# Odd K/V weight slabs: the low-part subtraction on GpSimd instead of VectorE, and the gated norm's squares taken step by step

## The chip, the cores and the metric

The kernel runs on one core of one Trainium2 chip. The metric is the device time of one execution in microseconds. Three runs of the kernel before gave 1953.63, 1960.84 and 1962.93 us (median 1960.84 us).

## What is computed

One layer of a hybrid decoder for 256 prompt tokens and 8 x 4 sample tokens (288 columns, T). A combined input projection feeds three mixers (conformer convolution, S5, Mamba-2 SSD), then come the output projection, cross-attention over 256 memory tokens, and a convolutional FFN. What matters here, cut from the reference:

```python
memn = _rmsnorm(mem_prompt, norm_mem_w[l])
mk = (memn @ xa_wk[l]).reshape(bp, N_MEM, XA_HEADS, XA_HEAD_DIM)
mv = (memn @ xa_wv[l]).reshape(bp, N_MEM, XA_HEADS, XA_HEAD_DIM)
...
y = y.reshape(bt, L, D_C) * jax.nn.silu(z.astype(f32))
yg = y.reshape(bt, L, SSD_GROUPS, D_C // SSD_GROUPS)
yg = yg * lax.rsqrt(jnp.mean(yg * yg, axis=-1, keepdims=True) + EPS)
```

## The kernel before

**The K/V stage.** The products with `xa_wk` and `xa_wv` are computed in 64 weight slabs (`y` = 0 to 63, eight groups of eight; a slab is 128 x 1024 elements). Each weight is split in a high and a low part of type fp32r: `hi` is the rounded copy, `lo` = weight - `hi`. Per slab, ScalarE (ACT) copies `raw` to `khi` (`k_split`, L1566), VectorE (DVE) subtracts `khi` from `raw` into `raw_lo` (`k_split`, L2286), and TensorE (PE) does 12 matmuls in `kv_group`: high x high, high x low (`raw_lo`) and low activations x high, for two tiles of memory tokens. `khi` has two buffers, so ACT writes slab y only when PE is done with slab y-2 (`wait_used_A`); `raw` and `raw_lo` have four. PE waits once per slab, on `kw_lo`, before its first matmul of the slab.

**What is woven in.** Between slabs PE runs hooks (`hook_kv`) with the work of the SSD mixer. For head pair j (0 to 7) the SSD's steps stand at fixed slabs, given by `ssd_at`: `ssd_a(j)` after slab 12+6j, `ssd_b(j)` after slab 15+6j. Each engine has its own queue in program order, written out by hand. ACT and DVE have a loop over y with `k_split(y + 1)` at the head of step y, and the SSD's operations behind it. On ACT, `ssd_decay(j)` (exponentials, L1641, L1643) is at step 13+6j, `ssd_states(j)` at 14+6j; at step 13+6j the load of the next state waits for a store (`st_ssd`).

**GpSimd (POOL)** has two plain loops for this stage. The first runs over j: `dec` x `cb` (L640) and `decs` x `cbs` (L643) twice, when ACT has made the exponentials, then the state times its decay (L649). The second, behind it, runs over j again: the square of the gated tile `zs` (L656) and its addition to `ssq` or `sqt` (L657), each waiting for `gated`, which DVE signals in `ssd_b(j)` at step 15+6j. PE's `gate_sums` (after slab 60) needs all squares. POOL does nothing else between the S5 mixer's products (L624, L626) and the memset behind the gate sums (L670).

**Other names.** At step 5 DVE makes `xds` (L2337, `token_rows(2)`), which PE's `chunk_state(0)` multiplies after slab 6. The first two slabs of `w_out`, y = 64 and 65, are also split by `k_split` into `khi` and `raw_lo`.

Of the kernel before, what the change touches and what calls it, by code (L numbers as in the profile page):

```python
# [6 lines left out]
F32 = mybir.dt.float32  # L7
F32R = mybir.dt.float32r
ALU = mybir.AluOpType
# [23 lines left out]
YT = NH * HP // P  # L33
# [59 lines left out]
def hymba_step(nc, I, O):  # L93
# [3 lines left out]
    def S(name):  # L97
        name = PLACE.get(name, (name, 0))[0]
        if name not in sems:
            sems[name] = ctx.enter_context(nc.semaphore(name))  # L100
        return sems[name]

    def at(name, count):

        return S(name), count + PLACE.get(name, (name, 0))[1]
# [4 lines left out]
    with ctx:  # L110

        def sb(name, shape, dt=F32):
            return alloc(ctx, name, shape, dt)
# [21 lines left out]
        raw_lo = alloc(lev, "raw_lo", [P, 4, 1024], F32R)  # L135
        lev.close()
        raw = sb("raw", [P, 4, 1024])
# [22 lines left out]
        khi = alloc(lev, "khi", [P, 2, 1024], F32R)  # L160
# [178 lines left out]
        NKV = 8 * 8  # L339
# [27 lines left out]
        def ssd_at(y, first):  # L367

            j, r = divmod(y - first, SSD_STEP)
            return j if r == 0 and 0 <= j < YT else None  # L370
# [195 lines left out]
        def _(pool):  # L566
# [66 lines left out]
            me.link(pool.memset(sqt[:, :], 0.0))  # L633


            for j in range(YT):
                g = j // 4
                for h in range(2):
                    pool.wait_ge(*at("decay", 4 * j + 2 * h + 1))
                    pool.tensor_tensor(vsplit(dec[:, h, :], 2), vsplit(dec[:, h, :], 2),  # L640
                                       cb[:, :, g, :], ALU.mult).then_inc(S("mixed"), 1)
                    pool.wait_ge(*at("decay", 4 * j + 2 * h + 2))
                    pool.tensor_tensor(decs[:, h, :], decs[:, h, :], cbs[:, g, :], ALU.mult)\  # L643
                        .then_inc(S("mixed"), 1)

                pool.wait_ge(*at("eb_ready", j + 1))
                pool.wait_ge(*at("s0_T", 2 * j + 2))
                last = eb[:, P:P + NS].rearrange("p (b l) -> p b l", l=NL)[:, :, NL - 1]
                pool.tensor_tensor(s0[:, j % 2, :, :], s0[:, j % 2, :, :],  # L649
                                   last.unsqueeze(2).to_broadcast([P, NB, NST]), ALU.mult)\  # L650
                    .then_inc(S("s0_decayed"), 1)

            for j in range(YT):
                pool.wait_ge(*at("gated", j + 1))
                dst = ssq if j < 4 else sqt
                me.link(pool.tensor_tensor(hbuf[:, 1, :], zs[:, j, :], zs[:, j, :], ALU.mult))  # L656
                q = pool.tensor_tensor(dst[:, :], dst[:, :], hbuf[:, 1, :], ALU.add)  # L657
                if j % 4 == 3:
                    q.then_inc(S("gate_sq"), 1)
                    pool.wait_ge(*at("gate_sq", j // 4 + 1))  # L660
                else:
                    me.link(q)


            for n, ready in enumerate(("x_out", "x_o", "x_down")):
                if n == 0:
                    pool.wait_ge(*at("gate_mm", 2))
# [28 lines left out]
        def _(pe):  # L696
# [288 lines left out]
            def kv_group(g, hook):  # L985
                for s in range(8):
                    sl = NA + 8 * g + s
                    pe.wait_ge(*at("kw_lo", 8 * g + s + 1))
                    wh = khi[:, sl % 2, :].rearrange("p (k n) -> p k n", k=2)
                    wl = raw_lo[:, sl % 4, :].rearrange("p (k n) -> p k n", k=2)  # L990
                    for t in range(MT):
                        if s == 0 and g > 0:
                            pe.wait_ge(*at("kv_read", 2 * (g - 1) + t + 1))
                        if s == 0 and g == 0:
                            pe.wait_ge(*at("in_read", 28 + t + 1))
                        for kk in range(2):
                            k = 2 * s + kk
                            if g == 0 and t == 0:
                                pe.wait_ge(*at("m_lo", k + 1))
                            xh, xl = mhi[:, k, t * P:(t + 1) * P], mlo[:, k, t * P:(t + 1) * P]  # L1000
                            mm(B[t][:, :], xh, wh[:, kk, :], k == 0, False)
                            mm(B[t][:, :], xh, wl[:, kk, :], False, False)
                            q = mm(B[t][:, :], xl, wh[:, kk, :], False, k == KT - 1)
                        if s == 7:
                            q.then_inc(S("kv_acc"), 1)
                    if s < 7:
                        q.then_inc(S("kv_slab"), 1)
                    hook(8 * g + s)
# [912 lines left out]
        def _(v):  # L1921
# [361 lines left out]
            def k_split(y):  # L2283

                v.wait_ge(*at("kw_hi", y + 1) if y < NKV else at("w_hi", y - NKV + 1))
                tt(raw_lo[:, y % 4, :], raw[:, y % 4, :], khi[:, y % 2, :].bitcast(F32), ALU.subtract)\  # L2286
                    .then_inc(S("kw_lo" if y < NKV else "w_lo"), 1)
# [123 lines left out]
                    ALU.mult, ALU.mult).then_inc(S("gate_scaled"), 1)  # L2411

            for y in range(NKV):
                k_split(y + 1)
                if y < 4:
                    mem_lo(8 + 2 * y)
                    mem_lo(9 + 2 * y)
                conf_end(y)
                if y == TOKENS_AT + 1:
                    token_columns()  # L2420
                if TOKENS_AT + 2 <= y < TOKENS_AT + 5:
                    token_rows(y - TOKENS_AT - 2)
                if y in (STATES_AT, STATES_AT + 1):
                    chunk_state(y - STATES_AT)
                if y == STATES_AT + 2:
                    final_state()
                if y == CB_AT:
                    c_b()
                if y == CB_AT + 1:
                    sample_tokens()  # L2430
                j = ssd_at(y, SSD_AT)
                if j is not None:
                    ssd_a(j)
                j = ssd_at(y, SSD_AT + SSD_HALF)
                if j is not None:
                    ssd_b(j)
                j = ssd_at(y, SSD_AT + SSD_HALF + 1)
                if j is not None:
                    ssd_update(j)
                if y == GATE_AT:  # L2440
                    for g in range(2):
                        v.wait_ge(*at("gate_mm", g + 1))
                        if g == 0:
                            v.wait_ge(*at("gated", YT))
                        ts(rstd[:, :] if g == 0 else hbuf[:, 0, :], B[2 + g][:, 0:T], 1.0 / 512, EPS,
                           ALU.mult, ALU.add).then_inc(S("gate_read"), 1)
                if y in (GATE_AT + 1, GATE_AT + 2):
                    gate_root(y - GATE_AT - 1)
                if y == NKV - 1:
                    for j in range(4):  # L2450
                        gate_scale(j)
# [304 lines left out]
```

## Time and profile before

| | |
|---|---|
| median of three runs | 1960.84 us |
| the profiled execution, whole time | 1955.62 us |
| its span | 1953.6 us |
| PE busy | 1893.7 us (97%) |
| DVE busy | 1088.5 us (56%) |
| ACT busy | 703.8 us (36%) |
| POOL busy | 235.2 us (12%) |

Everything is read from one profiled execution. Its span runs from its first to its last instruction; 2.0 us of the whole time lie around it. A wait is put down to the operation that released it last. Matmuls are pipelined, so that a row of 0.39 us is followed by the next 0.23 us later. PEclk is TensorE's granted clock, 1.00 for 2.4 GHz and 0.50 for 1.2 GHz. The timeline has one row for an instruction or a run of like ones: start, length, engine, line, operation, output <- inputs, count, and in brackets how long the engine sat idle before it and who ended that.

### The profile page before, as it was taken

How to read it: one execution, taken by the hardware profiler on the slowest of the kernel's cores; microseconds unless marked ns; L12 is line 12 of the kernel's file. 1: busy time of each engine (PE TensorE's matmuls, PEld its weight loads, DVE VectorE, ACT ScalarE, POOL GpSimd, SP SyncE). 2: the span in 40 equal slices, each digit the busy share in tenths (PEclk: the TensorE clock that was granted, in tenths of full speed). 3: DMA queues.
4: the chain of work that ended last, by engine and by line, in shares of the span. 5: the costliest groups of instructions: out<-in, count | busy, mean ns of one | idle time of the engine just before them, and what ended most of it. 6: DMA issues, size and time to landing. Idle time of an engine off the chain costs nothing.

```text
span 1953.6 us, 32075 instructions
## 1 busy us (share of the span) xinstructions
PE 1893.7 (97%) x12311; PEld 1690.9 (87%) x12311; DVE 1088.5 (56%) x1923; ACT 703.8 (36%) x1051; POOL 235.2 (12%) x257
## 2 busy tenths in 40 slices
PE   7999999799999999999999999999999999999998
PEld 4866677677777799996599999999999999999997
DVE  4796697564444546444334655555555554555554
ACT  2100152533333334324223444444444434444444
POOL 1023200001122233000013100000000000002300
PEclk9999999999999899999999999999999999999999
DMA  6333363355455646646745455555555555554553
GB/s 203 98 97 91 93 199 110 99 161 163 153 169 172 210 154 218 223 159 259 294 136 163 149 164 167 165 161 163 166 165 161 163 157 162 160 163 156 160 166 105
DMA packets 157953, 316.43 MB, mean 162 GB/s; under 512 B 16938, under 2 KB 39482, under 8 KB 152931
## 3 DMA queue, kind: packets, MB, share of 16 engines
q1 hardware_dynamic: 136146, 296.01, 48.6%
q10 hardware_dynamic: 21723, 19.27, 3.1%
q8 instruction: 56, 0.92, 0.2%
q14 instruction: 28, 0.23, 0.0%
HBM read 300.78 MB, written 14.89 MB: 162 GB/s over the span
## 4 chain that ended last, share of the span: by engine, by line
PE 86%; DVE 3%; ACT 2%; DMA 1%; issue 0%; ACTq 0%; SPq 0%; DVEq 0%
PE bank L698 23%; PE bank L1119 19%; PE bank L1121 19%; PE bank L1120 19%; PE bank L1219 2%; PE bank L1231 1%; PE bank L767 1%; PE bank L752 1%; DVE wlo L2459 1%; PE bank L1241 1%; DVE raw_lo L2286 1%; DMA raw<-in_w_out 1%; PE bank L1062 0%; DMA kv<-in_cache_mem_v 0%; DVE hlo L2481 0%
## 5 line engine op out<-in xcount | busy, mean ns | idle before, releaser
L1119 PE MATMUL bank<-hhi,whi 128*128 128x288 f32 x2128 | 635.4, 299 | 13.0 <-DVE wlo L2459 9.8
L1120 PE MATMUL bank<-hlo,whi 128*128 128x288 f32 x2128 | 632.0, 297 | 0.0
L1121 PE MATMUL bank<-hhi,wlo 128*128 128x288 f32 x2128 | 629.8, 296 | 0.0
L2459 DVE TENSOR_TENSOR wlo<-raw,whi 128x1024 fp32r<-128x1024 f32 (+1 forms) x270 | 330.3, 1224 | 390.0 <-ACT whi L1612 389.7
L1612 ACT ACTIVATE whi<-raw 128x1024 fp32r<-128x1024 f32 (+1 forms) x270 | 283.2, 1049 | 520.8 <-PE bank L1121 509.2
L1119 PEld LDWEIGHTS bank<-hhi,whi 128*128 128x128 f32 x2128 | 402.1, 189 | 14.9 <-DVE wlo L2459 14.6
L1121 PEld LDWEIGHTS bank<-hhi,wlo 128*128 128x128 f32 x2128 | 404.6, 190 | 0.0
L1120 PEld LDWEIGHTS bank<-hlo,whi 128*128 128x128 f32 x2128 | 402.9, 189 | 0.1
L698 PE MATMUL bank<-hT,raw 128*128 128x288 f32 x1024 | 264.7, 418 | 1.2 <-DVE hT L1946 1.2
L698 PEld LDWEIGHTS bank<-hT,raw 128*128 128x128 f32 x1024 | 196.9, 195 | 60.4 <-issue 7.4
L1119 PE MATMUL bank<-ahi,whi 128*128 128x288 f32 x688 | 204.3, 297 | 3.5 <-DVE alo L2696 1.6
L1120 PE MATMUL bank<-alo,whi 128*128 128x288 f32 x688 | 203.5, 296 | 0.0
L1121 PE MATMUL bank<-ahi,wlo 128*128 128x288 f32 x688 | 203.5, 296 | 0.0
L2693 DVE TENSOR_TENSOR wlo<-raw,whi 128x1024 fp32r<-128x1024 f32 x86 | 106.4, 1238 | 137.2 <-ACT whi L1888 137.1
L1888 ACT ACTIVATE whi<-raw 128x1024 fp32r<-128x1024 f32 x86 | 91.2, 1060 | 159.6 <-PE bank L1121 159.6
L2286 DVE TENSOR_TENSOR raw_lo<-raw,khi 128x1024 fp32r<-128x1024 f32 x66 | 86.6, 1312 | 93.2 <-ACT khi L1566 93.0
L1119 PEld LDWEIGHTS bank<-ahi,whi 128*128 128x128 f32 x688 | 129.3, 188 | 4.8 <-issue 2.8
L1120 PEld LDWEIGHTS bank<-alo,whi 128*128 128x128 f32 x688 | 129.3, 188 | 0.0
L1121 PEld LDWEIGHTS bank<-ahi,wlo 128*128 128x128 f32 x688 | 129.3, 188 | 0.0
L698 PE MATMUL bank<-khi,mhi 128*128 128x512 f32 x256 | 112.4, 439 | 13.0 <-DVE raw_lo L2286 12.9
L1566 ACT ACTIVATE khi<-raw 128x1024 fp32r<-128x1024 f32 x66 | 69.8, 1058 | 150.2 <-PE bank L698 146.3
L698 PE MATMUL bank<-raw_lo,mhi 128*128 128x512 f32 x256 | 106.6, 416 | 0.0
(474 smaller groups left out, 1978.9 us busy)
## 6 DMA issues: line engine op xcount, KB each, us to landing
raw<-in_ffn_w_down SPq DMA_DIRECT2D x86, 512.0 KB, 3.7
raw<-in_ffn_w_gate SPq DMA_DIRECT2D x80, 512.0 KB, 3.6
raw<-in_ffn_w_up SPq DMA_DIRECT2D x80, 512.0 KB, 3.6
raw<-in_w_in SPq DMA_DIRECT2D x64, 512.0 KB, 3.6
raw<-in_xa_wk SPq DMA_DIRECT2D x32, 512.0 KB, 3.8
raw<-in_xa_wv SPq DMA_DIRECT2D x32, 512.0 KB, 4.4
raw<-in_w_out SPq DMA_DIRECT2D x32, 512.0 KB, 3.8
raw<-in_xa_wq SPq DMA_DIRECT2D x32, 512.0 KB, 3.8
```

The costliest lines, as they stand in the source:

```text
L698: return pe.matmul(out, lhsT=l, rhs=r, start=start, stop=stop)
L752: q = pe.matmul(B[4 + j % 2][:, i * NP:(i + 1) * NP], lhsT=l, rhs=uT[r:r + 32, j // 4, 0:NP], start=True, stop=True, tile_position=(r, 0))
L1119: pe.matmul(out, lhsT=wh[:, wo:wo + P], rhs=xh, start=first, stop=False)
L1120: pe.matmul(out, lhsT=wh[:, wo:wo + P], rhs=xl, start=False, stop=False)
L1121: return pe.matmul(out, lhsT=wl[:, wo:wo + P], rhs=xh, start=False, stop=last)
L1219: x = pe.transpose(B[5 + u % 3][:, hh * NM + t * P:hh * NM + (t + 1) * P], cache(b)[:, t, c0:c0 + P], ident[:, :])
L1566: a(khi[:, y % 2, :], raw[:, y % 4, :], ACT.Copy).then_inc(S("kw_hi" if y < NKV else "w_hi"), 1)
L1612: a(whi[:, slot, 0:2 * width], raw[:, s % 4, 0:2 * width], ACT.Copy).then_inc(S("w_hi"), 1)
L1888: a(whi[:, slot, :], raw[:, n % 4, :], ACT.Copy).then_inc(S("w_hi"), 1)
L2286: tt(raw_lo[:, y % 4, :], raw[:, y % 4, :], khi[:, y % 2, :].bitcast(F32), ALU.subtract)\
L2459: tt(wlo[:, s % 2, wsl], raw[:, s % 4, wsl], whi[:, s % 2, wsl].bitcast(F32), ALU.subtract)\
L2693: tt(wlo[:, slot, :], raw[:, (NB_DOWN + base + j) % 4, :], whi[:, slot, :].bitcast(F32), ALU.subtract).then_inc(S("w_lo"), 1)
```

## The change

The subtractions `raw_lo` = `raw` - `khi` of the odd slabs (y = 1, 3, ... 63) are issued on POOL and leave DVE; the even ones stay. PE waits for `kw_lo_pool` at odd slabs and for `kw_lo` at even ones. POOL's two loops over j become one loop over y, with the SSD's steps at the slabs of the other engines' loops: `k_split` of the next slab at even steps, `ssd_mix(j)` at 13+6j, `s0_decay(j)` at 14+6j, `gate_square(j)` at 16+6j. The arithmetic is the same.

```diff
--- before.py
+++ after.py
@@ -633,7 +633,13 @@
             me.link(pool.memset(sqt[:, :], 0.0))
 
 
-            for j in range(YT):
+            def k_split(y):
+
+                pool.wait_ge(*at("kw_hi", y + 1))
+                pool.tensor_tensor(raw_lo[:, y % 4, :], raw[:, y % 4, :], khi[:, y % 2, :].bitcast(F32),
+                                   ALU.subtract).then_inc(S("kw_lo_pool"), 1)
+
+            def ssd_mix(j):
                 g = j // 4
                 for h in range(2):
                     pool.wait_ge(*at("decay", 4 * j + 2 * h + 1))
@@ -643,6 +649,7 @@
                     pool.tensor_tensor(decs[:, h, :], decs[:, h, :], cbs[:, g, :], ALU.mult)\
                         .then_inc(S("mixed"), 1)
 
+            def s0_decay(j):
                 pool.wait_ge(*at("eb_ready", j + 1))
                 pool.wait_ge(*at("s0_T", 2 * j + 2))
                 last = eb[:, P:P + NS].rearrange("p (b l) -> p b l", l=NL)[:, :, NL - 1]
@@ -650,7 +657,7 @@
                                    last.unsqueeze(2).to_broadcast([P, NB, NST]), ALU.mult)\
                     .then_inc(S("s0_decayed"), 1)
 
-            for j in range(YT):
+            def gate_square(j):
                 pool.wait_ge(*at("gated", j + 1))
                 dst = ssq if j < 4 else sqt
                 me.link(pool.tensor_tensor(hbuf[:, 1, :], zs[:, j, :], zs[:, j, :], ALU.mult))
@@ -661,7 +668,18 @@
                 else:
                     me.link(q)
 
-
+            for y in range(NKV - 1):
+                if y % 2 == 0:
+                    k_split(y + 1)
+                j = ssd_at(y, SSD_AT + 1)
+                if j is not None:
+                    ssd_mix(j)
+                j = ssd_at(y, SSD_AT + 2)
+                if j is not None:
+                    s0_decay(j)
+                j = ssd_at(y, SSD_AT + SSD_HALF + 1)
+                if j is not None:
+                    gate_square(j)
             for n, ready in enumerate(("x_out", "x_o", "x_down")):
                 if n == 0:
                     pool.wait_ge(*at("gate_mm", 2))
@@ -985,7 +1003,7 @@
             def kv_group(g, hook):
                 for s in range(8):
                     sl = NA + 8 * g + s
-                    pe.wait_ge(*at("kw_lo", 8 * g + s + 1))
+                    pe.wait_ge(*at("kw_lo_pool" if s % 2 else "kw_lo", (8 * g + s) // 2 + 1))
                     wh = khi[:, sl % 2, :].rearrange("p (k n) -> p k n", k=2)
                     wl = raw_lo[:, sl % 4, :].rearrange("p (k n) -> p k n", k=2)
                     for t in range(MT):
@@ -2411,7 +2429,8 @@
                     ALU.mult, ALU.mult).then_inc(S("gate_scaled"), 1)
 
             for y in range(NKV):
-                k_split(y + 1)
+                if y % 2:
+                    k_split(y + 1)
                 if y < 4:
                     mem_lo(8 + 2 * y)
                     mem_lo(9 + 2 * y)
```

## Rows read from the trace of the kernel before

**Rows 1.** Windows view, K/V stage: window, length, PE PEld DVE ACT POOL, PEclk, DMA, GB/s.
```profile
361.80:662.50 300.70, 284.15 (x1294) 213.71 (x1292) 151.08 (x218) 118.35 (x191) 51.80 (x57) 0.93 0.49 152
```

**Rows 2.** Waits of PE, 355 to 670 us: total us, times, longest.
```profile
PE bank L698 <- DVE raw_lo L2286: 12.9, 7, 5.5
PE bank L1119 <- DVE raw_lo L2286: 0.7, 1, 0.7
```

**Rows 3.** Timeline, slabs 27 and 28: start us, length us, engine, operation.
```profile
487.90 1.04 ACT L1566 ACTIVATE khi<-raw 128x1024 fp32r<-128x1024 f32 x1
489.12 1.22 POOL L643 TENSOR_TENSOR decs<-decs,cbs 32x32 f32<-32x32 f32 x1
490.32 1.91 POOL L649 TENSOR_TENSOR s<-s,eb 128x1024 f32<-128x1024 f32 x1
488.98 1.26 DVE L2286 TENSOR_TENSOR raw_lo<-raw,khi 128x1024 fp32r<-128x1024 f32 x1 [4.07 <-ACT khi L1566]
491.06 2.25 DVE L2286 TENSOR_TENSOR raw_lo<-raw,khi 128x1024 fp32r<-128x1024 f32 x1 [0.82 <-ACT khi L1566]
```

**Rows 4.** Timeline of PE: first matmul of slabs 1, 27, 33, 57 and 60.
```profile
368.56 0.50 PE L698 MATMUL bank<-khi,mhi 128*128 128x512 f32 x1 [0.86 <-DVE raw_lo L2286]
490.30 0.50 PE L698 MATMUL bank<-khi,mhi 128*128 128x512 f32 x1 [0.85 <-DVE raw_lo L2286]
520.20 0.50 PE L698 MATMUL bank<-khi,mhi 128*128 128x512 f32 x1 [2.02 <-DVE raw_lo L2286]
631.54 0.50 PE L698 MATMUL bank<-khi,mhi 128*128 128x512 f32 x1 [1.53 <-DVE raw_lo L2286]
649.44 0.50 PE L698 MATMUL bank<-khi,mhi 128*128 128x512 f32 x1 [0.27 <-DVE raw_lo L2286]
```

**Rows 5.** The subtractions on DVE: ns min/median/max, first and last start.
```profile
L2286 DVE TENSOR_TENSOR raw_lo<-raw,khi x66: 1201/1226/2248, 362.9 to 664.0; 128x1024 fp32r<-128x1024 f32 x66
```

**Rows 6.** The same view of five operations on POOL.
```profile
L643 POOL TENSOR_TENSOR decs<-decs,cbs x16: 242/244/1229, 430.9 to 630.4; 32x32 f32<-32x32 f32 x16
L640 POOL TENSOR_TENSOR dec<-dec,cb x16: 714/730/2027, 430.1 to 629.7; 128x256 f32<-128x256 f32 x16
L603 POOL TENSOR_TENSOR sqt<-xT x40: 666/668/1592, 692.8 to 1810.0; 128x288 f32<-128x288 f32 x40
L624 POOL TENSOR_TENSOR hAB<-gri,tabC x16: 1262/1264/1278, 128.7 to 229.4; 128x512 f32<-128x512 f32 x16
L649 POOL TENSOR_TENSOR s<-s,eb x8: 1905/1911/1919, 434.9 to 631.6; 128x1024 f32<-128x1024 f32 x8
```

**Rows 7.** Timeline near 642 us: DVE reading a PSUM bank beside POOL.
```profile
641.94 1.27 DVE L2400 TENSOR_TENSOR s<-bank,s 128x512 f32<-128x512 f32 x2
642.62 0.80 POOL L657 TENSOR_TENSOR sqt<-sqt,hbuf 128x288 f32<-128x288 f32 x1
```

**Rows 8.** Timeline, slab 15: ACT, DVE, PE.
```profile
432.57 1.06 ACT L1566 ACTIVATE khi<-raw 128x1024 fp32r<-128x1024 f32 x1 [2.06 <-PE bank L698]
433.66 1.23 DVE L2286 TENSOR_TENSOR raw_lo<-raw,khi 128x1024 fp32r<-128x1024 f32 x1 [3.31 <-ACT khi L1566]
435.11 0.40 PE L698 MATMUL bank<-khi,mhi 128*128 128x512 f32 x1
```

**Rows 9.** Timeline around the first chunk state: ACT, DVE, PE.
```profile
399.68 1.06 ACT L1566 ACTIVATE khi<-raw 128x1024 fp32r<-128x1024 f32 x1 [2.83 <-PE bank L698]
401.60 1.20 DVE L2337 TENSOR_TENSOR xds<-xdt,tokT 128x1024 f32<-128x1024 f32 x1
403.31 1.02 PE L698 MATMUL bank<-xds,btok 128*128 128x512 f32 x2
```

**Rows 10.** PE's wait in w_out; windows behind it and behind slab 33's start.
```profile
678.51 0.40 PE L1119 MATMUL bank<-hhi,whi 128*128 128x288 f32 x1 [2.98 <-DVE wlo L2459]
680.00:683.30 3.30, 3.30 (x15) 3.30 (x15) 0.00 (x0) 0.00 (x0) 0.00 (x0) 0.50 0.93 294
520.20:523.00 2.80, 2.80 (x12) 2.17 (x12) 2.03 (x1) 0.74 (x1) 1.92 (x2) 1.00 1.07 349
```

## The prediction

> **What bounds the kernel now.** First the busy shares of the page (the table above): TensorE (PE) 97%, everything else under 60%. Next the windows view of the K/V stage, slabs 0 to 63, the only part that the change touches: PE is busy for 284 of 300.7 us, DVE for 151, ACT for 118, POOL for 52 [rows 1]. So the stage is PE's, and DVE's busy time is worth nothing in itself. The waits of PE come third: those for L2286 are 12.9 us in seven in the stage and 0.7 us in one at the first slab of w_out [rows 2]. No wait of PE for POOL stands in that view. The timeline then tells what these waits are. At slabs 27, 33 and 57 `khi` itself is late (ACT had other work), and `raw_lo` follows at once: at slab 27 `khi` ends at 488.94, DVE subtracts from 488.98 to 490.24, PE starts at 490.30 [rows 3, 4]. None of the seven comes from DVE being busy with something else (at slab 60 its subtraction itself was held up, below); where DVE's queue held a subtraction back, PE had time in hand. The length of the subtraction itself is on PE's path wherever little time lies between the end of `khi` and PE's need.
>
> **The price of the new operation.** On DVE 66 subtractions take 1.226 us in the median [rows 5]. POOL does none of this kind in the trace. Its rows with two different full inputs are 0.730 us for 256 elements and 1.264 us for 512 [rows 6]: 2.09 ns an element and about 0.2 us fixed, which gives 1.264 + 512 x 0.00209 = 2.33 us for 1024. A row with 1024 elements is there, L649, at 1.911 us, but its second input is one value for 128 elements each; the square L603, both of whose inputs are the same tile, is cheap in the same way (0.668 us at 288, where the line of the other two gives 0.80). I take 2.33 us, since `raw` and `khi` differ in each element, and keep 1.91 as the lower end. Lower than that nothing in the trace suggests. The output type fp32r has no row on POOL, and neither has the way from POOL to PE; the trace has 0.04 us from ACT to DVE and 0.05 from DVE to PE [rows 3, 4], and I allow up to 0.15 more per hand-over as the upper end.
>
> The Trainium skill, "GPSIMD Engine Reference", section 3.1, has 4497 ns for a `tensor_tensor` add of 2048 fp32 elements on GpSimd, against 2293 on DVE. Half of it, 2.25 us, would be an estimate from that page for this operation; by it the ten delays below would each be 0.08 us shorter and the sum 0.8 us less. No run here shows that figure.
>
> **Who blocks whom.** At slab 27 POOL's small product starts at 489.12 and ends at 490.34, 0.10 us behind DVE's subtraction, where its median is 0.244 us [rows 3, 6]. Then DVE's subtraction of slab 28 starts at 491.06 and ends at 493.31, 1.08 us behind POOL's 490.32 to 492.23; it takes 2.25 us instead of 1.23 [rows 3]. So one stands still until the other is through. Both DVE subtractions read two tiles in SBUF. An operation of DVE that reads a PSUM bank and one SBUF tile, at 641.94, runs beside POOL's at 642.62, and both have their usual length (1.27 us for two, 0.80) [rows 7]; so I count collisions only where DVE reads two SBUF tiles. The Trainium skill, "SBUF — State Buffer", section "Who interferes with whom", says that a DVE instruction contends with a GpSimd one that reads SBUF if both its own inputs lie in SBUF; the rows agree; it speaks against this change, and without it the 0.9 us for `xds` below would fall away.
>
> **The change part by part.** Removed from DVE: 32 subtractions, 39 us, all beside PE's work: nothing. Added on POOL: 32 x 2.33 = 75 us, in a stage of 300 us where POOL has 52. What counts is each odd slab whose time from the end of `khi` to PE's start is less than 0.03 + 2.33 + 0.05 = 2.41 us. I went through all 32.
>
> - Slabs 1 and 3: PE already waits 0.86 and 5.5 us for DVE's result [rows 2, 4]. Each wait grows by 2.33 - 1.23 = 1.10 us: +2.2 us.
> - Slabs 15, 21, 39, 45: two slabs stand back to back without a hook between them. At slab 15 `khi` ends at 433.63, DVE is through at 434.89 and PE starts at 435.11, without a wait [rows 8]. The time is 1.48 us there and 1.45 to 1.49 at the other three. Each becomes a wait of 2.41 - 1.48 = 0.93 us: +3.7 us.
> - Slabs 27, 33, 51, 57: `khi` follows ACT's exponentials directly, and on POOL `ssd_mix(j)` stands ahead of `k_split(15+6j)`. At slab 27 its last product starts at 489.12 and takes 0.24 us when DVE is out of the way, so POOL is free at 489.36, 0.42 us behind the end of `khi`. The subtraction then ends at about 491.72 and PE starts at 491.77 instead of 490.30 [rows 3, 4]: +1.47 us. The same working gives 1.46 to 1.48 at 33, 51 and 57: +5.9 us. This is the only place where the order of POOL's queue costs something.
> - Slab 63: the same 1.48 us as slab 15, so +0.93; but slab 64, whose subtraction DVE can start earlier without slab 63's, had a wait of 0.7 us [rows 2] that absorbs most of it, while slab 65's `khi` hangs on slab 63's end and comes late. I take +0.5 us (0.05 to 0.93).
> - The first chunk state: `khi` of slab 7 ends at 400.74, so POOL works until 400.77 + 2.33 = 403.10. DVE's `xds`, two inputs in SBUF, wants to run from 401.60 to 402.80 and now ends 1.08 us behind POOL, at 404.18; PE wants it at 403.31 [rows 9]: +0.9 us.
> - The other odd slabs have 2.46 us or more and wait for nothing (25 and 49, at 2.46 to 2.48, have under 0.1 us to spare). DVE's subtraction for the next even slab may be held back behind POOL's at 16+6j, but those slabs have over 7 us.
> - The squares: 16 POOL operations leave the stretch 633 to 648 us and stand one by one behind `gated`. Behind `gate_square(j)` on POOL waits only slab 19+6j, whose `khi` comes 8 us later. What is won is the wait at slab 60, 0.27 us [rows 4], since there the squares held DVE's subtraction up: -0.27 us. No DMA and nothing on SP's queue moves.
>
> Nothing takes a delay back in between: what `khi` waits for is PE's own progress (`wait_used_A`), and the state's store is issued by PE's progress too. Sum: 2.2 + 3.7 + 5.9 + 0.5 + 0.9 - 0.3 = 12.9 us.
>
> **The clock.** After PE's wait of 2.98 us in w_out the granted clock was 0.50 from 680.0 to 683.3; after slab 33's 2.02 us it stayed at 1.00 [rows 10]. The waits at slabs 33 and 57 grow to about 3.5 and 3.0 us. A stretch of 3.4 us at half speed costs 1.7 us. I count one of the two: +1.7 us; bounds none and three (5.1 us).
>
> The forecast is +14.6 us: 1955.6 + 14.6 = 1970.2 us for the profiled execution. The median of the runs lies 5.2 us above that execution, so 1960.8 + 14.6 = 1975.4 us.
>
> **Rivals.**
> (a) *The subtraction costs POOL what L649 costs.* With 1.91 us the terms are 2 x 0.68, 4 x 0.51, 4 x 1.05, 0.45, 0.2 and -0.27: +8.0 us without a fall of the clock, 1968.9 us. For it: the only row of that size. Against it: the line through 256 and 512 elements, and L603.
> (b) *Relief of DVE decides, faster.* Where DVE does other work after `khi`, POOL starts at once; and the waits at slabs 60 and 64 go, 0.27 + 0.7 = 1.0 us [rows 2, 4]. That comes out ahead only if POOL's subtraction takes less than about 1.4 us, so that slabs 15 to 63 keep their cover: 1959.8 us. Against it: the rows of POOL at 512 elements and more [rows 6].
> (c) *Collisions breed more waits.* POOL is now busy for 75 us more, and each DVE operation with two SBUF inputs that meets it is held by up to 2.3 us; each hand-over costs 0.15 us more, slabs 25, 49 and 61 begin to wait, and the clock falls three times instead of once: 12.9 + 1.5 + 0.5 + 5.1 = +20.0 us, 1980.8 us. For it: the waits sit beside the hooks in which the clock falls already.
> That the change doesn't do what it says is no rival here: the line of each subtraction is fixed by the program.
>
> **Numbers.** Forecast 0.60, (a) 0.21, (b) 0.04, (c) 0.15. The range takes in (a) and (c) and, at each end, 3 us for the scatter of the runs (1953.6 to 1962.9): 1965 to 1984. About 0.5%, 9.8 us, is what a measurement of this kernel can tell from no change. The forecast and (c) lie beyond it, (a) within: slower 0.73, same 0.24, faster 0.03.
>
> **What would show it.** Right: POOL has 32 subtractions of about 2.3 us; PE's waits for POOL's subtraction stand at slabs 1, 3, 15, 21, 27, 33, 39, 45, 51, 57 and 63 and grow to 23 us or so with what was there; those at 27, 33 and 57 are 2.3, 3.5 and 3.0 us; PE waits some 0.9 us for `xds` near 405 us; slab 60 has no wait. The stage, 300.7 us, becomes 313 to 316 us, and what lies before and behind it keeps its length. Wrong: subtractions of 1.9 us or less (then it is (a)), or waits at slabs 5, 9, 17 or 23, which I hold to be covered.

## The result

The changed kernel takes 1983.4 us (median of four runs, 1981.9 to 1989.4) against 1961.9 us: the ratio is 1.0124, with a 95% interval of 1.0089 to 1.0159, slower by 17 to 31 us. Measured again beside others it was 1981.5 us (1972.1 to 1986.1, five runs), ratio 1.0096 (1.0080 to 1.0111). A ratio is taken over all the runs, not from the two medians (21.5 us apart in the first measurement). The forecast was +14.6 us; the first ratio stands for +24.3 us, the second for +18.8.

The page of the changed kernel, its first and its fourth part. Line numbers have moved: L716 is L698 of before, L1584 is L1566, L2304 is L2286, and POOL's subtraction is L639.

```profile
PE 1908.5 (96%) x12311; PEld 1698.5 (86%) x12311; DVE 1064.3 (54%) x1891; ACT 703.7 (36%) x1051; POOL 305.8 (15%) x289
PE bank L716 22%; PE bank L1137 19%; PE bank L1139 18%; PE bank L1138 18%; PE bank L1237 2%; POOL raw_lo L639 1%; PE bank L1249 1%; PE bank L770 1%; PE bank L785 1%; DMA out_s_ssd<-s 1%; DVE wlo L2478 1%; PE bank L1259 1%; DMA raw<-in_w_out 1%; PE bank L1080 0%; ACT khi L1584 0%
```

(The first line: busy us and share of each engine; the second: shares of the span by line in the chain that ended last.) POOL has 306 us of work instead of 235. DVE has only 24 us less, though 32 subtractions of 1.226 us, 39 us, have left it: those that are left take 1.68 us each in the mean of the stage, as some stand behind POOL's operations (below). POOL's `raw_lo` now stands in the chain with 1%. PE is busy for 1908.5 us instead of 1893.7, with the same 12311 instructions.

The windows view (window, length, busy us of PE, PEld, DVE, ACT, POOL, granted clock, DMA share, GB/s) of the kernel before and then of the changed one, each cut at the first `khi` and at the first matmul of w_out. The first line of the kernel before answers to [rows 1] with that cut.

```profile
361.80:662.56 300.76, 284.15 (x1295) 213.75 (x1293) 151.14 (x218) 118.35 (x191) 51.80 (x57) 0.93 0.49 152
0.00:361.80 361.80, 347.36 (x1505) 254.71 (x1506) 257.77 (x663) 70.39 (x142) 46.52 (x65) 0.98 0.42 128
662.56:1999.00 1336.44, 1262.17 (x9514) 1222.44 (x9514) 679.62 (x1043) 515.04 (x719) 136.88 (x135) 0.99 0.54 168
```

```profile
361.88:691.33 329.45, 299.64 (x1294) 222.10 (x1293) 127.79 (x188) 118.27 (x191) 122.11 (x89) 0.89 0.45 139
0.00:361.88 361.88, 346.66 (x1505) 254.13 (x1506) 257.78 (x663) 70.42 (x142) 46.57 (x65) 0.98 0.42 128
691.33:1999.00 1307.67, 1262.20 (x9514) 1222.28 (x9514) 678.71 (x1040) 514.99 (x719) 137.10 (x135) 0.99 0.55 172
```

(The last window runs past the end of the span.) The loss lies in the K/V stage alone: 300.8 us became 329.5 us, and the stretches before and behind it kept their length (361.8 and 361.9; 1291.0 and 1290.6 to the end). Inside the stage PE is idle for 329.45 - 299.64 = 29.8 us, where it was 300.76 - 284.15 = 16.6: +13.2 us. And it is busy for 15.5 us more with the same matmuls, at a granted clock of 0.89 instead of 0.93.

The second measurement has a profile of the changed kernel too. Its K/V stage:

```profile
360.76:682.23 321.47, 292.02 (x1295) 216.55 (x1293) 127.77 (x188) 118.25 (x191) 122.12 (x89) 0.91 0.46 143
```

Here the stage takes 8.0 us less than in the first profile, with as much idle time (29.5 us) and 7.6 us less of busy time, at a clock of 0.91. So the idle time is the kernel's, while the clock's part differs from one execution to the next.

The waits of PE (total us, times, longest), which answer to [rows 2]:

```profile
PE bank L716 <- POOL raw_lo L639: 23.3, 12, 6.4
PE bank L716 <- DVE raw_lo L2304: 1.9, 1, 1.9
PE bank L716 <- DVE xds L2355: 0.9, 1, 0.9
PE bank L1137 <- issue: 0.7, 1, 0.7
```

12.9 us in the stage became 23.3 + 1.9 + 0.9 = 26.1 us: +13.2, the idle time just found. The wait for `xds` is new. (DVE's 1.9 us, at slab 0, was in the 12.9 us already.)

POOL's subtraction (ns min/median/max), beside [rows 5, 6], and its collision at slab 9:

```profile
L639 POOL TENSOR_TENSOR raw_lo<-raw,khi x32: 2337/2367/2979, 367.5 to 685.1; 128x1024 fp32r<-128x1024 f32 x32
414.26 2.98 POOL L639 TENSOR_TENSOR raw_lo<-raw,khi 128x1024 fp32r<-128x1024 f32 x1 [8.19 <-ACT khi L1584]
```

2.37 us in the median, and never under 2.34. POOL started 0.07 to 0.14 us behind the end of `khi` where it was free, DVE 0.04 us [rows 3].

The timeline (start, length, engine, line, operation): the chunk state, beside [rows 9]; slab 15, beside [rows 8]; slab 27 and the start of slab 33, beside [rows 3, 4]:

```profile
404.45 2.71 DVE L2355 TENSOR_TENSOR xds<-xdt,tokT 128x1024 f32<-128x1024 f32 x1
407.21 1.13 PE L716 MATMUL bank<-xds,btok 128*128 128x512 f32 x2 [0.89 <-DVE xds L2355]
...
436.37 1.06 ACT L1584 ACTIVATE khi<-raw 128x1024 fp32r<-128x1024 f32 x1 [2.06 <-PE bank L716]
439.95 0.50 PE L716 MATMUL bank<-khi,mhi 128*128 128x512 f32 x1 [0.88 <-POOL raw_lo L639]
...
497.50 1.04 ACT L1584 ACTIVATE khi<-raw 128x1024 fp32r<-128x1024 f32 x1
498.73 0.24 POOL L649 TENSOR_TENSOR decs<-decs,cbs 32x32 f32<-32x32 f32 x1
498.94 2.34 POOL L639 TENSOR_TENSOR raw_lo<-raw,khi 128x1024 fp32r<-128x1024 f32 x1
501.24 1.90 POOL L656 TENSOR_TENSOR s<-s,eb 128x1024 f32<-128x1024 f32 x1
500.65 3.58 DVE L2304 TENSOR_TENSOR raw_lo<-raw,khi 128x1024 fp32r<-128x1024 f32 x1 [6.46 <-ACT khi L1584]
501.33 0.50 PE L716 MATMUL bank<-khi,mhi 128*128 128x512 f32 x1 [2.34 <-POOL raw_lo L639]
...
534.17 0.80 PE L716 MATMUL bank<-khi,mhi 128*128 128x512 f32 x1 [3.46 <-POOL raw_lo L639]
```

At slab 27 `khi` ends at 498.54, POOL is still at its last product until 498.94, and PE starts 2.34 us late; at slab 33 it is 3.46 us, at slab 15 0.88 us. DVE's `xds` took 2.71 us instead of 1.20, as POOL's subtraction of slab 7 (403.67 to 406.07) was in the way. The 3.58 us of DVE's subtraction for slab 28 are the same thing: it ends 1.09 us behind POOL's state product (501.24 to 503.14). PE did not need it yet.

The clock behind the waits, in the windows view: behind the start of slab 27, behind that of slab 33 and in the slab behind the next hook. The third number from the end is the granted clock.

```profile
501.00:505.00 4.00, 3.67 (x10) 2.91 (x11) 3.23 (x1) 0.00 (x0) 2.15 (x2) 0.62 0.33 124
534.20:540.00 5.80, 5.80 (x16) 4.18 (x16) 2.88 (x1) 0.24 (x1) 1.79 (x1) 0.54 0.23 84
547.30:553.00 5.70, 5.70 (x15) 4.44 (x15) 2.41 (x3) 0.13 (x1) 0.00 (x0) 0.50 0.00 0
```

Behind the wait of 3.46 us PE worked at or near 1.2 GHz (0.54) for slab 33's twelve matmuls, where the kernel before had 1.00 at the same place [rows 10]. Behind 2.34 us it was 0.62. Yet a wait alone does not settle the clock. The second profile of the changed kernel, behind the same wait at slab 33 (3.45 us):

```profile
532.70:538.50 5.80, 5.80 (x35) 4.60 (x36) 2.90 (x1) 1.06 (x1) 3.37 (x2) 1.00 0.47 156
```

And slab 0, where nothing has changed yet and both kernels wait alike (1.88 us before, 1.89 now): the stretch from its start in the kernel before, then in the changed one, and the changed kernel's slab 1.

```profile
364.20:368.50 4.30, 3.47 (x16) 2.67 (x16) 3.63 (x7) 3.81 (x9) 0.00 (x0) 1.00 0.03 5
364.30:368.60 4.30, 4.30 (x12) 3.29 (x13) 2.44 (x6) 3.03 (x7) 1.13 (x1) 0.64 0.00 0
369.89 0.50 PE L716 MATMUL bank<-khi,mhi 128*128 128x512 f32 x1 [0.53 <-POOL raw_lo L639]
```

The same length of wait was followed by full speed once and by the low clock once. At slab 1 the slow matmuls of slab 0 took up most of the time for which PE would have waited: 0.53 us are left, while the slab starts 2.56 us behind the end of its `khi` instead of 1.31 us.

### The profile page after: what moved, and what is told of

The parts are those of the page before. It is cut to its first block, busy times and chain, and to the rows that moved or that the text cites. A ratio compares the mean times of both kernels' runs of the same rounds, so it can differ in the third digit from the quotient of the medians.

```text
span 1981.9 us, 32075 instructions
## 1 busy us (share of the span) xinstructions
PE 1908.5 (96%) x12311; PEld 1698.5 (86%) x12311; DVE 1064.3 (54%) x1891; ACT 703.7 (36%) x1051; POOL 305.8 (15%) x289
## 4 chain that ended last, share of the span: by engine, by line
PE 85%; DVE 2%; ACT 2%; POOL 2%; DMA 2%; issue 1%; ACTq 0%; SPq 0%; DVEq 0%; POOLq 0%
PE bank L716 22%; PE bank L1137 19%; PE bank L1139 18%; PE bank L1138 18%; PE bank L1237 2%; POOL raw_lo L639 1%; PE bank L1249 1%; PE bank L770 1%; PE bank L785 1%; DMA out_s_ssd<-s 1%; DVE wlo L2478 1%; PE bank L1259 1%; DMA raw<-in_w_out 1%; PE bank L1080 0%; ACT khi L1584 0%
## 5 line engine op out<-in xcount | busy, mean ns | idle before, releaser
L1137 PE MATMUL bank<-hhi,whi 128*128 128x288 f32 x2128 | 634.7, 298 | 12.9 <-DVE wlo L2478 9.8
L1137 PEld LDWEIGHTS bank<-hhi,whi 128*128 128x128 f32 x2128 | 401.9, 189 | 14.9 <-DVE wlo L2478 14.6
L716 PE MATMUL bank<-hT,raw 128*128 128x288 f32 x1024 | 263.1, 415 | 1.2 <-DVE hT L1964 1.2
L716 PEld LDWEIGHTS bank<-hT,raw 128*128 128x128 f32 x1024 | 195.6, 194 | 60.1 <-issue 7.4
L716 PE MATMUL bank<-khi,mhi 128*128 128x512 f32 x256 | 117.6, 460 | 25.3 <-POOL raw_lo L639 23.3
L1584 ACT ACTIVATE khi<-raw 128x1024 fp32r<-128x1024 f32 x66 | 69.8, 1057 | 169.7 <-PE bank L716 165.8
L639 POOL TENSOR_TENSOR raw_lo<-raw,khi 128x1024 fp32r<-128x1024 f32 x32 | 76.4, 2389 | 290.3 <-ACT khi L1584 290.3
L694 POOL TENSOR_TENSOR cg<-cg,rstd 128x288 f32<-128x288 f32 x43 | 42.9, 998 | 482.9 <-ACT cg L1856 482.9
```

Of the source, the lines that this page charges most:

```text
L639: pool.tensor_tensor(raw_lo[:, y % 4, :], raw[:, y % 4, :], khi[:, y % 2, :].bitcast(F32), ALU.subtract).then_inc(S("kw_lo_pool"), 1)
L694: pool.tensor_tensor(cg[:, m, :], cg[:, m, :], rstd[:, :], ALU.mult)\
L716: return pe.matmul(out, lhsT=l, rhs=r, start=start, stop=stop)
L1137: pe.matmul(out, lhsT=wh[:, wo:wo + P], rhs=xh, start=first, stop=False)
L1584: a(khi[:, y % 2, :], raw[:, y % 4, :], ACT.Copy).then_inc(S("kw_hi" if y < NKV else "w_hi"), 1)
```

## The experiments

For the experiments a second measure helps. Each run of each kernel has its span and its mean granted clock. Their product is the time that the run would take at full clock, if all of it scaled; the remainder of the span is what the clock cost. (A wait that falls into a stretch at half clock counts at half its length there, so the split is not exact.) The means over the runs of each kernel, with the standard error in brackets:

| kernel | runs | median us | ratio to before (95%) | span x clock | clock's cost |
|---|---|---|---|---|---|
| before | 54 | 1962.6 | 1 | 1914.3 (0.2) | 46.9 (0.6) |
| changed (both measurements) | 9 | 1982.3 | see above | 1926.1 (0.6) | 54.1 (2) |
| squares alone | 10 | 1961.1 | 0.9978 (0.9958 to 0.9998) | 1912.7 (0.7) | 45.4 (1.4) |
| longer on VectorE | 4 | 1987.1 | 1.0126 (1.0109 to 1.0143) | 1927.0 (1.0) | 59.1 (1.7) |
| waits filled | 4 | 1977.8 | 1.0075 (1.0054 to 1.0096) | 1928.4 (1.0) | 46.9 (1.9) |
| twelve slabs on VectorE | 10 | 1959.0 | 0.9985 (0.9971 to 0.9999) | 1914.6 (0.5) | 43.3 (1.2) |
| high parts first, GpSimd | 12 | 1954.1 | 0.9957 (0.9939 to 0.9975) | 1911.1 (0.5) | 40.7 (0.9) |
| high parts first, VectorE | 6 | 1950.6 | 0.9944 (0.9923 to 0.9965) | 1908.0 (0.4) | 40.6 (1.3) |
| split before mix | 4 | 1983.2 | 1.0114 (1.0088 to 1.0140) | 1924.5 (0.8) | 56.5 (1.9) |
| before, filled | 10 | 1961.5 | 1.0001 (0.9983 to 1.0019) | 1920.1 (0.4) | 40.6 (0.9) |
| four late slabs on VectorE | 6 | 1971.2 | 1.0041 (1.0027 to 1.0056) | 1921.4 (0.7) | 47.6 (1.6) |
| seven short ones on VectorE | 7 | 1972.8 | 1.0046 (1.0023 to 1.0069) | 1918.9 (0.7) | 51.2 (2.3) |

So over nine runs the change costs 11.8 us of full-clock time and 7.2 (2) us of clock. In the one profiled pair the clock's part looks like 15 us, mostly because the profiled execution of the kernel before was a lucky one: 1953.6 x (1 - 0.979) = 41 us of clock's cost, where 54 runs have 46.9 in the mean.

My theory after the result: the waits are as forecast; what the forecast missed is the clock, which PE's idle time costs. The rivals: GpSimd's work slows PE in another way; or one of the change's parts does something that I had not seen.

**1. The squares alone.** All subtractions on VectorE, GpSimd's loops merged. The lines below are against the changed kernel, and cut; PE waits for `kw_lo` at every slab again.

```diff
-                if y % 2 == 0:
-                    k_split(y + 1)
                 j = ssd_at(y, SSD_AT + 1)
...
-                if y % 2:
-                    k_split(y + 1)
+                k_split(y + 1)
```

> The step-by-step squares alone; all subtractions stay on VectorE. Theory (the loss is PE's waits for GpSimd's subtractions and the low clock behind them): the wait at slab 60 (0.27 us) goes and nothing else moves, 1961 us, within 2 us of the kernel before, PEclk of the K/V stage 0.93. Rival (the squares, spread over the stage, hold VectorE and so PE up at many slabs): slower by 3 us or more, with waits of PE that the kernel before has not.

Measured: 1961.1 us, 0.9978 (0.9958 to 0.9998). In full-clock time it is 1.6 us less than the kernel before. PE's waits in its profile:

```profile
PE bank L708 <- DVE raw_lo L2296: 13.8, 7, 5.1
```

There is no new kind of wait. The squares cost nothing; if anything they bring a little. In this one execution the seven waits sum to 13.8 us, so the 0.27 us of slab 60 can't be seen in the sum: where a slab's `khi` comes late by itself, its wait differs between executions (1.58 us here at slab 27 against 0.85, 0.64 at slab 51 where the kernel before had none).

**2. The same delay without GpSimd's subtractions.** The kernel before, with idle work on VectorE.

```diff
+        EXTRA = {**{y: (940,) for y in (1, 3, 15, 21, 39, 45, 63)}, **{y: (940, 200) for y in (27, 33, 51, 57)}}
...
             def k_split(y):
                 v.wait_ge(...)
+                for n in EXTRA.get(y, ()):
+                    me.link(v.reduce_max(xsum[:, 0, 0:1], raw[:, y % 4, 0:n], axis=AX.X))
```

> The kernel before, with idle work on VectorE (a reduce_max into a scratch column) ahead of the subtraction of the eleven odd slabs at which the changed kernel makes PE wait (1, 3, 15, 21, 27, 33, 39, 45, 51, 57, 63), about 1.0 us long, at 27, 33, 51 and 57 about 1.4 us. GpSimd does not take part. Theory: PE's waits for raw_lo grow by some 11 us, and the granted clock of the K/V stage falls from 0.93 to about 0.89, so that the whole is 20 to 26 us slower, 1981 to 1987 us. Rival (the low clock comes from GpSimd's reading, not from the waits): only the waits, 10 to 12 us slower, 1971 to 1974 us, clock 0.93.

Measured: 1987.1 us, 1.0126 (1.0109 to 1.0143), the upper end of what was expected. Stage, waits and two rows of the timeline:

```profile
362.11:698.24 336.13, 301.05 (x1294) 223.54 (x1293) 170.61 (x233) 118.19 (x191) 52.74 (x57) 0.87 0.44 136
PE bank L699 <- DVE raw_lo L2289: 31.4, 13, 6.4
498.03 1.91 POOL L650 TENSOR_TENSOR s<-s,eb 128x1024 f32<-128x1024 f32 x1 [0.86 <-ACT s0T L1658]
498.35 2.67 DVE L2289 TENSOR_TENSOR raw_lo<-raw,khi 128x1024 fp32r<-128x1024 f32 x1
```

The waits grew by 18.5 us, not 11, so the size can't be compared to a microsecond. The last two lines, at slab 27, show why: the delayed subtraction met POOL's state product, which the kernel before has too, and took 2.67 us instead of 1.23. The same happened at 33, 51 and 57, some 1.4 us each. The kind can be compared: no subtraction ran on GpSimd, and the clock's cost rose from 46.9 to 59.1 us. (The 0.87 is that of the slowest of the four runs.) That the low clock needs GpSimd's subtractions is ruled out.

**3. The waits filled.** The changed kernel, with unused matmuls ahead of PE's wait. They write bank 5; the wait for `gated` holds them until VectorE has read it.

```diff
+        FILL = {15: 3, 21: 3, 27: 9, 33: 14, 39: 3, 45: 3, 51: 12, 57: 12}
...
+                    if 8 * g + s in FILL:
+                        if 8 * g + s > 15:
+                            pe.wait_ge(*at("gated", (8 * g + s - 15) // 6))
+                        for _ in range(FILL[8 * g + s]):
+                            mm(B[5][:, :], mhi[:, 0, 0:P], mhi[:, 0:2, :].rearrange("p k n -> p (k n)"))
                     pe.wait_ge(*at("kw_lo_pool" if s % 2 else "kw_lo", (8 * g + s) // 2 + 1))
```

> The changed kernel, with matmuls whose results nobody uses (3 to 14 of them, about 0.23 us each) ahead of PE's wait at slabs 15, 21, 27, 33, 39, 45, 51 and 57, as long as the waits they fill. What PE waits for is unchanged. Theory: the low clock came with the idle time, so most of the 13.6 us of added PE time in the stage comes back: 1968 to 1976 us, clock of the stage 0.92 or more. Rival: the low clock has another cause, and the time stays at 1983 us, within 3 us.

Measured: 1977.8 us, 1.0075 (1.0054 to 1.0096).

```profile
361.59:690.10 328.51, 309.56 (x1353) 229.34 (x1352) 128.02 (x188) 118.23 (x191) 122.27 (x89) 0.90 0.45 140
PE bank L717 <- POOL raw_lo L640: 12.5, 12, 6.6
```

The kernel does more work and is at least no slower: in the mean 1977.5 against 1982.3 us, but with an error of 2.5 on the difference, and the ratios' intervals overlap. The clock's cost fell from 54.1 to 46.9 us (7.2, with an error of 2.7), that of the kernel before, while the full-clock time rose by 2.3 us: the fillings are 59 x 0.23 = 13.6 us, and the waits that they took the place of 23.3 - 12.5 = 10.8. The median is a little above the range that I gave; and in the profiled execution the clock of the stage is 0.90, not the 0.92 that I expected. Only the mean over the runs shows the effect.

**4. Twelve slabs back on VectorE.**

```diff
+        ON_DVE = (1, 3, 7, 15, 21, 27, 33, 39, 45, 51, 57, 63)
+        def on_pool(y):
+            return y % 2 == 1 and y < 64 and y not in ON_DVE
...
-                    pe.wait_ge(*at("kw_lo_pool" if s % 2 else "kw_lo", (8 * g + s) // 2 + 1))
+                    pe.wait_ge(*lo_at(8 * g + s))
```

> The changed kernel, but the eleven slabs with little time between khi and PE's need, and slab 7 (whose subtraction holds up xds), go back to VectorE; the other 20 odd slabs stay on GpSimd. Theory: their subtractions are covered, PE's waits are those of the kernel before without slab 60's, 1959 to 1963 us, clock 0.93. Rival (GpSimd's subtractions cost PE time wherever they run): 20 of 32 are left, so over half of the 21 us, 1972 us or more.

Measured: 1959.0 us, 0.9985 (0.9971 to 0.9999).

```profile
361.18:670.92 309.74, 292.97 (x1295) 216.73 (x1293) 128.75 (x198) 118.24 (x191) 97.84 (x77) 0.90 0.48 148
PE bank L725 <- DVE raw_lo L2313: 13.0, 6, 5.1
```

Twenty subtractions on GpSimd cost nothing, and PE does not wait for POOL at all: the whole loss sits at the twelve slabs that the prediction named. There is no gain either. The stage's clock in this execution is 0.90 too, against 0.93 in the profile of the kernel before, and yet over ten runs the clock's cost is 3.6 (1.3) us lower than that kernel's, with the same 13 us of waits. So one execution's clock in one stage is no measure, and something besides the length of the waits moves the clock's cost by a few microseconds.

**5 and 6. High parts first.** PE waits for `khi`, does the eight matmuls that need only `khi`, and only then waits for `raw_lo`. Once with the change (5), once with all subtractions on VectorE and the squares step by step (6). The lines are those of (5), cut; in (6) the second wait is for `kw_lo`.

```diff
-                    pe.wait_ge(*at("kw_lo_pool" if s % 2 else "kw_lo", (8 * g + s) // 2 + 1))
+                    pe.wait_ge(*at("kw_hi", 8 * g + s + 1))
...
                             mm(B[t][:, :], xh, wh[:, kk, :], k == 0, False)
-                            mm(B[t][:, :], xh, wl[:, kk, :], False, False)
-                            q = mm(B[t][:, :], xl, wh[:, kk, :], False, k == KT - 1)
+                            mm(B[t][:, :], xl, wh[:, kk, :], False, False)
+                    pe.wait_ge(*at("kw_lo_pool" if s % 2 else "kw_lo", (8 * g + s) // 2 + 1))
+                    for t in range(MT):
+                        for kk in range(2):
+                            k = 2 * s + kk
+                            q = mm(B[t][:, :], mhi[:, k, t * P:(t + 1) * P], wl[:, kk, :], False, k == KT - 1)
```

> The changed kernel with TensorE's order in a K/V slab turned: it waits for khi, does the eight matmuls that need only khi (about 1.9 us), and waits for raw_lo before the last four. Theory: at slabs 15, 21, 39, 45 and 63 GpSimd's 2.4 us are covered (1.48 + 1.9 us), at 3, 27, 33, 51 and 57 a wait of about 0.5 us is left of 0.9 to 3.5, only khi's own lateness counts; the waits in the stage fall from 26 to some 10 us, 1957 to 1966 us. Rival (the waits are not what costs): 1975 us or more.

> The same order of matmuls, all subtractions on VectorE, squares step by step. Theory: 1.23 us are covered everywhere; of the kernel before's 12.9 us of waits 6 to 7 go, 1952 to 1957 us, faster than the kernel before and than the same order with GpSimd by 2 to 6 us. Rival (GpSimd's help pays once its length is covered): the one with GpSimd is the faster of the two.

Measured: 1954.1 us, 0.9957 (0.9939 to 0.9975) with GpSimd, and 1950.6 us, 0.9944 (0.9923 to 0.9965) with VectorE. First the stage and the waits of (5), then of (6):

```profile
360.35:658.56 298.21, 284.70 (x1294) 213.55 (x1293) 125.94 (x187) 117.73 (x191) 123.38 (x89) 0.93 0.50 154
PE bank L716 <- ACT khi L1588: 4.5, 2, 4.2
PE bank L716 <- POOL raw_lo L639: 1.7, 3, 0.7
PE bank L716 <- DVE xds L2359: 0.9, 1, 0.9
```

```profile
361.47:655.27 293.80, 282.62 (x1294) 211.98 (x1293) 149.75 (x218) 117.61 (x191) 57.07 (x57) 0.93 0.51 156
PE bank L708 <- ACT khi L1580: 4.8, 2, 4.5
```

Both came out a little below their ranges. Waits of 2.4 us in all for `vtok` and `zs` are new in both; with them PE waits some 10 us in the stage in (5), as expected. With the same subtractions on GpSimd, PE's waits for them fall from 23.3 to 1.7 us, and the loss of 20 us turns into a gain of 8. It was the place of the wait in PE's order that made the length count. GpSimd's help is still worth nothing: in full-clock time (5) is 3.1 us behind (6), of which 1.7 + 0.9 us stand in the waits. (6) is the fastest kernel of this study, 12 us ahead of the kernel before: 6.3 us less at full clock and 6.3 us less of clock's cost.

**7. GpSimd's subtraction ahead of the mix.**

```diff
-                if y % 2 == 0:
+                if y % 2 == 0 and ssd_at(y, SSD_AT + 2) is None:
                     k_split(y + 1)
                 j = ssd_at(y, SSD_AT + 1)
                 if j is not None:
+                    k_split(y + 2)
                     ssd_mix(j)
```

> The changed kernel, with GpSimd's subtraction of slab 15+6j put ahead of ssd_mix(j). Theory: at slabs 27, 33, 51 and 57 the 0.42 us that it stood behind the products goes, so these waits shrink by 0.4 us each, and nothing else: 1.7 us less than the changed kernel, 1981 to 1982 us, or the same within the scatter. Rival (the order of GpSimd's queue is the main loss): over 6 us less. Second rival (the products, now behind, hold up ssd_b): new waits of PE for dec or decs.

Measured: 1983.2 us, 1.0114 (1.0088 to 1.0140).

```profile
PE bank L717 <- POOL raw_lo L639: 22.5, 12, 6.5
```

0.8 us less of waits than the changed kernel in the profile, 1.6 (1.0) us less at full clock, and nothing to be seen in the median. At slabs 33 and 57 the waits are 3.15 and 2.68 us instead of 3.46 and 2.96; no wait for `dec` or `decs` came. The order of POOL's queue is a small term, as forecast; the length is the large one.

**8. The kernel before, filled.** As (3), but with all subtractions on VectorE and `FILL = {15: 4, 21: 4, 39: 4, 45: 4, 27: 10, 33: 15, 51: 6, 57: 13}`.

> The kernel before, all subtractions on VectorE, with unused matmuls ahead of the same eight slabs: as much time as GpSimd's longer subtraction costs there (4 to 15 of 0.23 us, 13.6 us in all, of which about 4 us fill waits that are there already), with no idle time of PE. Theory (only the matmul engine's idle time lowers the clock): PEclk of the stage 0.93 or more, the time 1962 + 9.6 = 1970 to 1973 us. Rival (the low stretches behind ssd_b's small matmuls get longer when the slabs' times shift, idle or not): clock 0.90 to 0.91, 1976 to 1980 us.

Measured: 1961.5 us, 1.0001 (0.9983 to 1.0019).

```profile
361.62:678.48 316.86, 305.12 (x1354) 229.67 (x1353) 151.46 (x218) 118.18 (x191) 51.84 (x57) 0.90 0.47 145
678.48:1999.00 1320.52, 1256.36 (x9514) 1217.87 (x9514) 679.37 (x1043) 514.95 (x719) 137.70 (x135) 0.99 0.54 170
PE bank L699 <- DVE raw_lo L2292: 8.1, 4, 5.1
```

Both expectations missed on the time; the stage's clock in the profile, 0.90, is the rival's. The 60 more matmuls lengthen the stage by 16.1 us in the profile, and cost nothing in ten runs: 5.8 (0.4) us more at full clock, 6.3 (1.1) us less of clock's cost. So delays that are filled with work cost no clock, but give some back that the waits of the kernel before had cost already. Against the changed kernel it is 21 us faster, but that comparison is not even: slab 27 starts 1.81 us behind its `khi` here and 2.79 us there, slab 51 1.35 and 2.78, and slabs 1, 3 and 63 have no filling. Where in the span the clock comes back the profiles don't tell: behind the stage PE is busy for 1256.4 us here and for 1262.2 in the kernel before, but the two profiles of the changed kernel, 1262.2 and 1259.4, differ by half as much.

**9 and 10. Which waits cost the clock.** As (4), with `ON_DVE = (27, 33, 51, 57)` and with `ON_DVE = (1, 3, 15, 21, 39, 45, 63)`. The changed kernel ran again beside them (11).

> The changed kernel with only slabs 27, 33, 51 and 57 back on VectorE, whose waits were 2.3 to 3.5 us. Their part of the waits is 5.9 us. Theory (the long waits bring the low clock, the short ones don't): these 5.9 us and most of the clock's part go, 1968 to 1972 us. Rival (each wait costs clock in proportion, or the stage's length alone decides): half of the whole loss stays, 1973 to 1976 us.

> The changed kernel with the other seven tight slabs (1, 3, 15, 21, 39, 45, 63) back on VectorE, the four late ones left on GpSimd. Their part of the waits is about 6.4 us. Theory: only these 6.4 us go, and the clock's part stays: 1976 to 1979 us, that is 5 us or more above the kernel with the four late ones on VectorE. Rival: both kernels come out alike, 1973 to 1976 us.

> The changed kernel once more, beside the two others, for its median and its clock over more runs: 1983 us, 20 to 22 us above the kernel before, PEclk of the K/V stage 0.88 to 0.90; about 13.8 us of it full-speed time (span times mean clock), the rest the clock.

Measured: 1971.2 us, 1.0041 (1.0027 to 1.0056), as expected; 1972.8 us, 1.0046 (1.0023 to 1.0069), under the 1976 to 1979 us that I expected; the changed kernel 1981.5 us, 18.5 above the kernel before (20 to 22 expected), 12.0 of it at full clock. The waits of (9), then of (10):

```profile
PE bank L725 <- POOL raw_lo L648: 11.4, 7, 6.5
PE bank L725 <- DVE raw_lo L2313: 7.8, 5, 2.0
```

```profile
PE bank L725 <- POOL raw_lo L648: 12.6, 4, 3.5
PE bank L725 <- DVE raw_lo L2313: 8.2, 3, 5.5
```

At full clock the four late slabs are worth 1926.1 - 1921.4 = 4.7 us (forecast 5.9), the seven others 7.2 us (forecast 2.2 + 3.7 + 0.5 = 6.4). Each has an error of 0.9. Together 11.9, all of the 11.8 us within the error, though the 0.9 us for `xds` are left in both kernels. The clock's cost falls by 6.5 (2.5) us with the first and by 2.9 (3) with the second. That points to the long waits, but the two kernels differ by 1.6 us in the median, where I expected 5 or more; that is nearer to the rival, by which both come out alike, and the errors overlap. Which waits bring the low clock stays open.

## Why the prediction was right or wrong

- **The price of the operation** was right: 2.33 us forecast, 2.37 measured. The line through 256 and 512 elements held, and L649 of the kernel before, the row nearest in size, would have misled: rival (a) is out. With its fp32r output the operation lies 0.04 us above the line from rows with f32 outputs. The estimate from the Trainium skill, "GPSIMD Engine Reference", section 3.1, was 2.25 us; the measurement decides for 2.37, 5% above it.
- **The waits** came at the slabs named and, but for two, in the sizes named: 6.44 us at slab 3 for 6.6; 0.88 us four times for 0.93; 2.34, 3.46 and 2.96 us at 27, 33 and 57 for 2.3, 3.5 and 3.0; 0.9 us for `xds`. Slab 1 had 0.53 us for the 1.96 that the working gives, since slab 0 ran at the low clock. Slab 51 had 2.89 us (2.31 in the second profile), where +1.47 had been forecast on no wait: the slab starts 2.78 us behind its `khi`, as forecast, but `khi` itself was late. ACT's exponentials ahead of it began 8.2 us after the state's store was issued (615.01 to 623.22), and 6.7 us in the kernel before (593.14 to 599.80). "Nothing takes a delay back" left out that this store's time varies. The sum was forecast as 12.9 us; it is 13.2 in the profile and 11.8 over nine runs. Experiments 4, 9 and 10 take it apart in the same pieces.
- **The blocking** was right, and the Trainium skill's rule in "SBUF — State Buffer", section "Who interferes with whom", agrees again: `xds` with its two SBUF inputs stood behind POOL (2.71 us for 1.20). Slab 9's subtraction on POOL was held up too (2.98 us), under cover, and so was DVE's of slab 28 (3.58 us).
- **The squares** were right: they cost nothing (experiment 1), and the wait at slab 60 is not there in the changed kernel's timeline. Slab 61 waits 0.27 us instead, which rival (c) had and the forecast had not.
- **The hand-over to w_out** was wrong by a little: I let slab 64's wait of 0.7 us absorb slab 63's 0.93. It is still there in the changed kernel, put down to "issue", so POOL's 0.88 us at slab 63 counted in full.
- **The step that failed is the clock**, a term that was mis-sized. I priced one stretch of 3.4 us after a wait of about 3 us, 1.7 us in all, with 5.1 us as the bound. Over nine runs it is 7.2 (2) us, and in the profiled pair about 15. With it the stage, forecast at 313 to 316 us, took 329.5 and 321.5 us in the two profiles. The working took two rows, one wait with a fall behind it and one without [rows 10], as a threshold, and counted only the waits near it. The traces have no such threshold: 1.88 and 1.89 us at slab 0 gave 1.00 and 0.64, and 3.46 and 3.45 us at slab 33 of the same kernel gave 0.54 and 1.00. The kernel before loses 46.9 us to low clock in a run already, and what was missing is how this cost moves when PE idles more everywhere. Rival (c) had the size (+20 us), and partly by luck. Its 5.1 us of clock are nearest to the 7.2. The further collisions came as well (of 39 us taken from DVE only 24 were gained), and the hand-over from ACT to POOL was 0.03 to 0.10 us longer than that to DVE. But PE waited for almost none of this: 0.27 us at slab 61, and nothing at 25 and 49.
- **The base.** I took the profiled execution as it was. It was one with less of clock's cost (41 us) than the mean (46.9), so that a comparison of two profiles alone shows 28 us where the runs show 19 to 24. The four runs beside which the change was first measured were low too, 1960.2 us in the mean against 1963.1 for the 54: 3 of the first +24.3 us are that.
- **The range** ended at 1984 us. The first ratio, set on the median of 1960.8, gives 1985.2, just above; the second gives 1979.7, inside.

What is shown: the waits and their causes, and that idle time of PE costs clock in the mean of many runs (3 against the changed kernel, 8 against the kernel before, 2 without GpSimd's subtractions). What is not: where in the span the cost comes back, which waits bring it, and what else moves it (experiment 4).

## What to carry to other kernels

Before moving an operation to a slower engine because that engine is free, list for each use how long it may take between its input and its reader's need; here 20 of 32 had room and 12 had not, and DVE's relief was worth nothing, since DVE was not what PE waited for. Where the reader has work that doesn't need the late operand, turn its order first: that gave 12 us, more than any choice of engine. And price a wait of TensorE at more than its length: here each microsecond lost at full clock cost some 0.6 us more in the clock (7.2 of 11.8 us), as a mean over nine runs. In the experiments it was between 0.1 (four late slabs on VectorE) and 1.0 (longer on VectorE), so this is a rough figure for this kernel.

## What the runs showed of the hardware

- A GpSimd subtraction of two different 128 x 1024 tiles takes 2.34 to 2.41 us undisturbed; with one input constant over 128 elements the product takes 1.91 us.
- Matmuls that nobody needs, put where PE would have waited, lowered the changed kernel's clock cost by 7.2 (2.7) us, and sixty of them cost the kernel before nothing in time.
- Two executions of the same kernel, behind the same wait of PE (3.46 and 3.45 us at slab 33), had a granted clock of 0.54 and 1.00.
- A DVE subtraction with both inputs in SBUF that starts beside a POOL product ends some 1.1 us behind it: 2.67 and 3.58 us instead of 1.23.
- The clock's cost of one and the same kernel varies from run to run: 54 runs of the kernel before lie between 1956.4 and 1972.8 us, 4.1 us of standard deviation, while span times clock lies between 1910.6 and 1917.1 us, with 1.6. For a comparison of a few microseconds the mean clock has to be read beside the time.
